# Sliding attention moved ahead of the forget attention in a two-layer hybrid block

## The reference

```
proj = rms_norm(h) @ w_in
fq, fk, fv, ff, cq, ckv, krope, sq, sk, sv, gates = split(proj)
log_decay = cumsum(log_sigmoid(ff + fox_forget_b))
out_a = causal_attention(norm(fq), norm(fk), fv, log_decay)      # forget branch, 8 heads of 64
q, k, v = up-projections of norm(cq), norm(ckv), with rope
out_b = causal_attention(norm(q), norm(k), v)                    # latent branch, 8 heads of 96
out_c = sliding_window(norm(sq), norm(sk), sv, sinks, alibi)     # 8 query heads, 2 shared key heads
y = einsum(branches, w_branch);  merged = sum(sigmoid(gates) * y)
h = h + merged @ w_o
u = rms_norm(h) @ w_up;  h = h + (silu(conv(gate)) * conv(val)) @ w_down
```

## Time and profile before

| | us |
|---|---|
| median of 3 runs | 2052.18 |
| lowest and highest of them | 2051.9 and 2056.09 |
| the profiled execution, its own time | 2050.07 |
| its span in the profile | 2048.3 |
| TensorE busy, share of the span | 1974.3, 96% |
| mean granted TensorE clock | 0.992 |

### The profile page before, as it was taken

One profiled execution on the slowest core, in us unless ns is written; L12 is line 12 of the kernel. 1 busy time (PEld: TensorE's weight loads), 2 busy tenths in 40 slices (PEclk: granted clock), 3 DMA queues, 4 the chain that ended last, 5 costly groups with the idle time before them and its releaser, 6 DMA issues.

```text
span 2048.3 us, 37777 instructions
## 1 busy us (share of the span) xinstructions
PE 1974.3 (96%) x15080; PEld 1876.6 (92%) x15080; DVE 1154.7 (56%) x2137; ACT 766.3 (37%) x1483; POOL 1019.4 (50%) x1306
## 2 busy tenths in 40 slices
PE   7899999999999999999998999999999999999999
PEld 7888898888999999999997888988889999999999
DVE  5665466677455665652256654666774656656411
ACT  5455566555232222220034555665552232222100
POOL 5745544444444444455467555444443445444543
PEclk9999999999999999999999999999999999999999
DMA  4212111111233323323332121111112323232332
GB/s 154 56 50 63 52 44 61 45 50 52 63 105 93 93 83 94 93 83 104 93 115 63 43 63 53 52 52 52 52 42 73 115 83 102 85 100 87 103 94 93
DMA packets 44803, 156.35 MB, mean 76 GB/s; under 512 B 5010, under 2 KB 5266, under 8 KB 44628
## 3 DMA queue, kind: packets, MB, share of 16 engines
q1 hardware_dynamic: 44484, 153.71, 24.8%
q10 hardware_dynamic: 144, 0.22, 0.0%
HBM read 149.58 MB, written 4.26 MB: 75 GB/s over the span
## 4 chain that ended last, share of the span: by engine, by line
PE 80%; DVE 10%; ACT 4%; issue 3%; POOL 2%; DMA 0%; DVEq 0%; ACTq 0%; SPq 0%; POOLq 0%
PE ps L1294 22%; PE ps L1297 21%; PE ps L1299 21%; PE ps L1528 5%; PE ps L1304 3%; DVE osum L1906 2%; PE ps L1435 1%; PE ps L1474 1%; DVE rstd L1619 1%; DVE ps L1876 1%; POOL wl L789 1%; PE ps L1480 1%; PE ps L1500 1%; DVE square L1614 1%; ACT square L987 1%
## 5 line engine op out<-in xcount | busy, mean ns | idle before, releaser
L789 POOL TENSOR_TENSOR wl<-raw,wh 128x256 fp32r<-128x256 f32 x1080 | 797.8, 771 | 723.5 <-DVE wh L1598 714.0
L1294 PE MATMUL ps<-xh,wh 128*128 128x264 f32 (+1 forms) x2880 | 810.6, 303 | 4.9 <-POOL wl L789 2.7
L1297 PE MATMUL ps<-xl,wh 128*128 128x264 f32 (+1 forms) x2880 | 762.9, 285 | 0.0
L1299 PE MATMUL ps<-xh,wl 128*128 128x264 f32 (+1 forms) x2880 | 584.1, 284 | 0.0
L1294 PEld LDWEIGHTS ps<-xh,wh 128*128 128x128 f32 x2880 | 545.5, 189 | 29.0 <-issue 16.0
L1297 PEld LDWEIGHTS ps<-xl,wh 128*128 128x128 f32 x2880 | 545.8, 190 | 15.4 <-issue 6.7
L1299 PEld LDWEIGHTS ps<-xh,wl 128*128 128x128 f32 x2880 | 450.4, 190 | 0.0
L1598 DVE CAST wh<-raw 128x1024 fp32r<-128x1024 f32 x270 | 200.2, 742 | 180.7 <-PE ps L1294 166.2
L1297 PE MATMUL ps<-al,wh 128*128 128x264 f32 (+1 forms) x704 | 184.9, 283 | 0.0
L1294 PE MATMUL ps<-ah,wh 128*128 128x264 f32 (+1 forms) x704 | 183.6, 283 | 0.0
L1898 DVE TENSOR_TENSOR ps<-ps,cst 128x128 f32<-128x128 f32 (+6 forms) x240 | 70.9, 296 | 189.0 <-PE ps L1480 135.8
(11 more groups left out here) (183 smaller groups left out, 3213.3 us busy)
## 6 DMA issues: line engine op xcount, KB each, us to landing
raw<-weights SPq DMA_DIRECT2D x270, 512.0 KB, 3.6
h<-tokens SPq DMA_DIRECT2D x4, 528.0 KB, 6.6
h<-tokens SPq DMA_DIRECT2D x8, 264.0 KB, 5.4
residual<-h SPq DMA_DIRECT2D x8, 264.0 KB, 4.7
h<-residual SPq DMA_DIRECT2D x8, 264.0 KB, 5.9
out<-h SPq DMA_DIRECT2D x8, 256.0 KB, 4.9
cst<-constants SPq DMA_DIRECT2D x1, 1008.0 KB
extra<-positions SPq DMA_DIRECT2D x17, 4.1 KB
```

Of the source, the lines that this page charges most:

```text
L789: ins = nc.gpsimd.tensor_tensor(wl[c % SPLIT][:, part], raw[:, c % RAW, part], wh[c % SPLIT][:, part].bitcast(F32), ALU.subtract)
L1294: a = nc.tensor.matmul(out, a_hi, x_hi[:, sl], start=first, stop=False)
L1297: nc.tensor.matmul(out, a_hi, x_lo[:, sl], start=False, stop=False)
L1299: ins = nc.tensor.matmul(out, a_lo, x_hi[:, sl], start=False, stop=last)
```

## The change

The jobs are reordered: sliding 0 to 3, forget 4 to 7, latent 8 to 11. The first pair of tiles is now `ff` and `sk`, the shared keys of the sliding branch. The gates follow: the sliding branch's gates now lie in `merged`, the forget branch's in the ring `gsb`. `BEGIN`, `ORDER`, the leads and the lags are new numbers. GpSimd fills eight rows of each buffer in place of ten, and buffer 1's fills come 4 blocks after `ff` in place of 24; the rows of ones in `xq` are written by "extras2" for the first two jobs of either branch. The rows of positions for job 0 are loaded at block 3. "kfill" of jobs 0 and 1 waits for the fills of its buffer, and "PVM" of job 0 on ScalarE waits until the decay's rows are made, since both use `osum` and `oraw`.

```diff
--- before.py
+++ after.py
@@ -27,8 +27,8 @@
 BIG = 3.0e38
 PAIRS = HEADS // 2
 FOX, MLA, SWA = range(3)
-JOBS = [(FOX, p) for p in range(PAIRS)] + [(SWA, p) for p in range(PAIRS)] + [(MLA, p) for p in range(PAIRS)]
-FIRST_JOB = {FOX: 0, SWA: PAIRS, MLA: 2 * PAIRS}
+JOBS = [(SWA, p) for p in range(PAIRS)] + [(FOX, p) for p in range(PAIRS)] + [(MLA, p) for p in range(PAIRS)]
+FIRST_JOB = {SWA: 0, FOX: PAIRS, MLA: 2 * PAIRS}
 
 BLK = 8
 CW = BLK * P
@@ -79,14 +79,14 @@
 G_STORED_IN_H = {4: 0, 5: 1, 6: 4, 7: 5}
 Y_LAST = [4, 5, 6, 7, 0, 1, 2, 3]
 STAT_LAG, NORM_LAG = 2, 4
-BEGIN = [65, 94, 122, 156, 192, 221, 250, 280, 319, 354, 391, 436]
-ORDER = ("fk0 fv0 gF0 fq1 fk1 gF1 fk2 fq2 fv1 fk3 fv2 fq3 gF2 sq0 gF3 fv3 sk sv gF4 gF5 sq1 gF6 sq2 gF7 yF0 cq0 cq1 yF1 sq3 yF2 yF3 ckv yF4 mq0 yF5 mv0 yF6 mq1 yF7 gS0 mk0 gS1 mv1 mq2 gS2 gS3 mq3 yS0 mk1 yS1 mq4 gS4 gS5 mq5 yS2 mv2 mk2 gS6 mq6 yS3 gS7 yS4 yS5 mq7 yS6 mk3 gM2 mv3 gM5 gM0 gM4 gM6 yS7 gM1 gM7 gM3")
-M_LEAD, M_STEP, NT_LEAD = 25, 1.8, 4
+BEGIN = [56, 76, 107, 134, 169, 203, 245, 275, 343, 375, 413, 443]
+ORDER = ("sq0 sv sq1 gS0 gS1 sq2 gS2 gS3 sq3 gS4 fk0 gS5 fq0 fv0 gS6 fk1 gS7 fq1 yS0 fv1 yS1 yS2 fk2 yS3 fq2 yS4 yS5 fv2 fk3 yS6 fq3 yS7 fv3 cq0 cq1 ckv gF0 mv0 mq0 gF1 mq1 gF2 mv1 mk0 gF3 yF0 mq2 yF1 gF4 mq3 gF5 mk1 yF2 mq4 gF6 yF3 mq5 gF7 yF4 mv2 yF5 mk2 yF6 mq6 yF7 mq7 gM2 gM1 mk3 gM0 mv3 gM5 gM6 gM4 gM7 gM3")
+M_LEAD, M_STEP, NT_LEAD = 25, 1.9, 3
 ST_HEAD, PV_LAG, ST_END = 7, 2, 13
-ZEROS = 10
-FIRST_LEAD, FIRST_STEP = 18, 1.0
-START = [13, 16, 11, 25, 25, 29, 12]
-LAG = {("dve", "layer stat"): 1, ("dve", "M"): 1, ("dve", "MM"): 1, ("act", "O"): -1, ("pool", "high"): -1, ("act", "head copy"): 1, ("dve", "STM"): -1, ("dve", "decay2"): 2, ("pool", "extras2"): -1, ("dve", "rope"): -1, ("dve", "square low"): 1, ("act", "inverse"): 2}
+ZEROS = 8
+FIRST_LEAD, FIRST_STEP = 18, 0.8
+START = [13, 17, -12, 2, 25, 31, 3]
+LAG = {("dve", "layer stat"): 1, ("dve", "M"): 1, ("dve", "MM"): 1, ("pool", "high"): -1, ("act", "head copy"): 1, ("pool", "extras2"): -1, ("dve", "rope2"): 1, ("act", "kfill"): -1, ("dve", "square low"): -1, ("dve", "decay2"): 1, ("act", "PVM"): -1, ("act", "inverse"): 2, ("dve", "decay"): 1}
 
 
 def constants():
@@ -193,7 +193,7 @@
                 order.append((t, k))
 
     branch = {"F": FOX, "S": SWA, "M": MLA}
-    a, b = tile("ff"), tile("fq", 0)
+    a, b = tile("ff"), tile("sk")
     order.extend((t, k) for k in range(KD) for t in (a, b))
     for name in ORDER.split():
         kind, m = name.rstrip("0123456789"), int("0" + name.lstrip("abcdefghijklmnopqrstuvwxyzFSM"))
...
@@ -241,17 +241,18 @@
                 t.joint = tiles[t.i - 1]
             put(e + STAT_LAG, 3, "stat", t)
             at = e + NORM_LAG
-            job = {"fq": 0, "fk": 0, "sq": PAIRS, "mk": 2 * PAIRS}.get(t.kind)
+            job = {"fq": PAIRS, "fk": PAIRS, "sq": 0, "mk": 2 * PAIRS}.get(t.kind)
             job = t.m + job if job is not None else 2 * PAIRS + t.m // 2 if t.kind == "mq" else None
             if job is not None and job >= 2:
                 at = max(at, BEGIN[job - 2] + ST_END)
             put(at, 6, "newton", t)
             put(at + 1, 6, "norm", t, 0)
+            high_at[job] = at
             if t.kind in ("cq", "mk"):
                 put(at + 2, 6, "norm", t, 1)
             if t.kind == "mq":
                 put(e + 1, 6, "turn", t)
-            put(at + 2 + (START[-1] if t.m == 0 and t.kind == "fq" else 0), 7, "high", t)
+            put(at + 2 + (START[-1] if t.kind == "sk" else 0), 7, "high", t)
             assert next_in_slot[t.i] >= e + STAT_LAG + 1, (t.kind, t.m, next_in_slot[t.i] - e)
         if t.kind in ("fv", "sv", "mv"):
             put(e + 3, 3, *place(("VT", t, 0)))
@@ -266,7 +267,7 @@
                 put(e + at, rank, step, 0)
             for n in range(ZEROS):
                 put(1 + n, 8, "zero", 0, n)
-                put(e + 24 + n, 8, "zero", 1, n)
+                put(e + 4 + n, 8, "zero", 1, n)
             put(4, 9, "zero values")
             put(e + 2, 9, "zero low")
     for i, pairs in ((end_of["g", (FOX, 3)], ((FOX, 0), (FOX, 2))), (end_of["g", (FOX, 7)], ((FOX, 4), (FOX, 6))),
@@ -283,11 +284,12 @@
         elif j > 0:
             put(b - M_LEAD - 9, 4, "extras", j)
             put(b - M_LEAD - 5, 4, "extras2", j)
+        lead, by = (M_LEAD, M_STEP) if j else (FIRST_LEAD, FIRST_STEP)
         if br == SWA:
-            put(b - M_LEAD - 4, 7, "kfill", j, 0)
-            put(b - M_LEAD - 3, 7, "kfill", j, 1)
+            i = min(b - lead - 4, high_at[j])
+            put(i, 7, "kfill", j, 0)
+            put(i, 7, "kfill", j, 1)
         parts = [(e, q) for e in range(2) for q in (("4", "3", "2", "1") if br == SWA else ("4a", "4b", "3", "2", "1"))]
-        lead, by = (M_LEAD, M_STEP) if j else (FIRST_LEAD, FIRST_STEP)
         for n, (e, q) in enumerate(parts):
             put(b - lead + int(n * by), 4, *place(("M", j, e, q)))
         put(b - lead + int(len(parts) * by), 4, *place(("MM", j)))
...
@@ -806,7 +808,7 @@
 
             fills = [(t, lo, HD + lo, lo_e, 0, n, 0) for t, n in ((xq, T), (xk, TK)) for lo, lo_e in ((HD, 0), (0, 1))]
             fills += [(xk, 0, HD, 0, 0, 1, 0), (xk, HD, P, 1, 0, 1, 0), (xk, MQ, MQ + 1, 0, 0, TK, 1),
-                      (xk, 0, 1, 1, 0, TK, 1), (xq, HD, HD + 2, 0, 0, T, 1), (xq, 32, 34, 1, 0, T, 1)]
+                      (xk, 0, 1, 1, 0, TK, 1)]
             assert len(fills) == ZEROS
 
             def zero(i, n):
@@ -882,6 +884,8 @@
                                 nc.gpsimd.tensor_copy(xq[row:row + 2, i, e, :], extra[0:2, 0:T]).then_inc(
                                     pool_step.sem, pool_step.tick((l, "position", j, e)))
                                 began["last"] = (pool_step.sem, pool_step.n)
+                            elif br == FOX and p < 2:
+                                fill(xq, row, row + 2, i, e, 0, T, 1)
                         settled()
                         pool.sem_inc(extras_placed.sem, extras_placed.tick((l, j)))
                     elif s[0] == "ones":
...
@@ -1127,7 +1131,12 @@
                         j, e = s[1], s[2]
                         i, kv = j % 2, JOBS[j][1] // 2
                         src = slice(kv * HD, (kv + 1) * HD)
-                        act.wait_ge(scores_ready.sem, scores_ready.at(l, j - 2, 1, 4))
+                        if j >= 2:
+                            act.wait_ge(scores_ready.sem, scores_ready.at(l, j - 2, 1, 4))
+                        else:
+                            act.wait_ge(zeroed.sem, zeroed.at(l, j))
+                            if l > 0:
+                                act.wait_ge(spilled.sem, spilled.at(l - 1))
                         act.wait_ge(key_low.sem, key_low.at(l, "sk"))
                         own, other = slice(e * HD, (e + 1) * HD), slice((1 - e) * HD, (2 - e) * HD)
                         copy(xk[own, i, e, 1:T + 1], skh[src, :].bitcast(F32))
@@ -1216,6 +1225,8 @@
                     elif s[0] == "PVM":
                         j = s[1]
                         act.wait_ge(meta_done.sem, meta_done.at(l, j))
+                        if j == 0:
+                            act.wait_ge(decay_ready.sem, decay_ready.at(l))
                         if j > 0:
                             act.wait_ge(heads_low.sem, heads_low.at(l, j - 1))
                         bank = banks[s[2]["bank"]]
...
```

28 lines of the change are left out of this document (14 added, 14 removed).

## The result

The changed kernel takes **2109.36 us** (median of 4 runs, 2105.43 to 2112.44), the kernel before 2052.04 in the same comparison. The ratio is 1.0279, with a 95% interval of 1.0257 to 1.03: 57 us slower. The forecast was 2057.3, with a range up to 2067. The side was right, the size was wrong by a factor of ten.

A forecast was written before the change was run, and what follows sets the result against it. TensorE, busy 96% of the span, was taken as the bound. Terms -0.6 - 5.5 + 9.0 + 2.2 = +5.1 on 2050.07 gave 2055.2, raised by the profiled run's 2.1 below median to 2057.3 us; range 2043 to 2067.

The forecast's parts named there:

- The start, layer 0: Blocks up to 56 in layer 0: new waits of 11.2 us, plus 1.7 of low clock.
- the chain to the first scores: Layer 0 start: GpSimd and ScalarE queues delay job 0's first scores to 56.5; TensorE waits 4.7 us.
- the rule on the shared port: Start: two-input VectorE instructions block GpSimd's SBUF reads, so fills stay slow; without it the sum would be -7.6, not -0.6.
- the waits of 3.1 for a maximum behind it and of 2.4 behind rope: Layer 0 start: TensorE waits 3.1 us for maxima behind VectorE's scan, then 2.4 uncovered behind rope and a cast.
- That kind of wait: Start: first scores waiting for GpSimd to place the decay's rows; 7.4 of 7.7 us forecast to go.
- The start, layer 1: Layer 1 start: four copies replace two fills, chain about 1.2 us later, waits 12.4 us, plus 1.7 clock.
- the whole start: Start, both layers: 24.1 us comes and 24.7 goes, net -0.6; bounds -16 to +6.
- rival (a): Start pays, with no decay delaying first scores: -8 to -16 instead of -0.6, total 2042 to 2050; chance 0.26.
- The latent branch's first scores: Latent branch's start: wait for the key's high part goes, with its low clock; -5.5 us, at worst 0.
- The end of attention: Output tiles' fourth block waits 3.5 us per layer for job 11's heads; +9.0 with clock, bounds 6 to 12.
- Crowding: Latent jobs within blocks 343 to 443, and the sliding branch: small waits grow; +2.2 us, bounds -2 to +8.
- rival (d): ScalarE falls behind in sliding jobs, later starts cost wait plus low clock; +10 to +16, 2062 to 2068; chance 0.16.

The follow-up runs named there:

- e1: Changed kernel with VectorE's reciprocals of the four latent pairs cut to 4 of 132 columns; 20.5 us faster than the changed kernel.
- e4: Changed kernel with its last pair four blocks earlier and the last keys' tile two tiles earlier; median 4.6 us slower than the changed kernel, intervals overlapping.
- e11b: Changed kernel with the third latent pair's keys tile 9 blocks earlier, ahead of two forget output tiles; no measurable gain.
- e13: Changed kernel with eight tiles reordered at blocks 378 to 415, two latent gate tiles moved ahead; 8 us faster than the changed kernel.
- e15: Changed kernel with VectorE's reciprocals of the four sliding pairs cut to 4 of 132 columns; 15.9 us faster than the changed kernel.
- e12: Changed kernel with its start mended: decay, scan, rope, second buffer's zeros and first forget values later, shared keys' low half unmoved; 9.7 us faster.
- e8: Old kernel with two of four VectorE reciprocals of each latent pair done three times; 27.6 us slower than the old kernel.
- e18: Changed kernel with VectorE's reciprocals of all twelve pairs cut to 4 columns; 34.0 us faster than the changed kernel.
- e5: Changed kernel with latent tiles from block 305 ordered as in the old kernel and last pairs moved; time not stated, blocks 304 to 490 excess some 124 us.
- e16: Changed kernel with latent tiles earlier and spread, latent pairs at 333, 366, 400, 436, and the start mended; 2126 us.
- e3: Changed kernel with M_STEP and NT_LEAD put back to the old kernel's 1.8 and 4; 2113.81 us.

## Why the prediction was wrong

The terms in the order of the sum, both layers, against the excess of the table above.

- **The start, layer 0: the chain to the first scores right, the terms behind it wrong.** GpSimd's and ScalarE's queues in after:

```profile
34.66 0.88 POOL L879 CAST xk<-extra 2x530 fp32r<-2x530 f32 x1 [0.17 <-DMA extra<-positions]
...
44.39 1.31 POOL L804 CAST xq<-unit 64x528 fp32r<-64x528 f32 x2 [0.17 <-POOL yk L804]
...
47.83 1.74 POOL L924 TENSOR_TENSOR skl<-q,skh 128x528 fp32r<-128x528 f32 x1
```
```profile
49.66 0.65 ACT L974 ACTIVATE xk<-skh 64x528 fp32r<-64x528 f32 x1 [2.77 <-POOL skl L924]
...
53.24 0.73 ACT L1060 ACTIVATE oraw<-osum,prm 8x528 f32<-8x528 f32 x1
...
55.35 1.31 ACT L974 ACTIVATE xq<-q 64x528 fp32r<-64x528 f32 x2
```
```profile
52.47 0.66 PE L1409 MATMUL ps<-cst,vt 128*128 128x128 f32 x4 [2.64 <-DVE vt L1736]
53.70 0.27 PE L1414 MATMUL ps<-cst,vt 128*17 128x128 f32 x1
56.76 0.47 PE L1446 MATMUL ps<-xk,xq 66*128 66x16 f32 x2 [1.33 <-issue]
58.58 0.80 PE L1446 MATMUL ps<-xk,xq 66*128 66x16 f32 x2 [1.35 <-ACT vx L974]
...
76.33 0.47 PE L1446 MATMUL ps<-xk,xq 66*128 66x16 f32 x2 [1.61 <-POOLq L890]
```

The low part was forecast to end at 49.2 (49.57 here), ScalarE's six copies at 53.1 (53.2), the decay at 55.2 (55.3), the first scores at 56.5 (56.76). The four copies took 34.66 to 38.39, 3.7 for 3.9. The five fills were not slow, as I had them (4.2 us) and as I had expected by the rule on the shared port: they took 3.2, and VectorE stood idle beside them for 2.13 of these us:

```profile
46.92 0.71 DVE L1625 TENSOR_TENSOR square<-ssum,square 128x528 f32<-128x528 f32 x1 [2.13 <-ACT square L993]
```

The low part of the key, with VectorE at work beside it, took 1.74 for 1.31, and the queue had begun 0.8 later than I had it; so the close hit on 49.2 is in part luck. The wait of 4.7 us came in two pieces, 2.6 for the values behind the decay on VectorE and 1.3 for the scores, which I had taken for one. Behind it the prediction fails: the scan ended at 61.1, as forecast, but the waits of 3.1 for a maximum behind it and of 2.4 behind rope did not come. In their place stand 1.4 us for ScalarE's copy of the values (58.58) and 1.6 us for the position rows of job 1 on GpSimd (76.33). That kind of wait I had counted as gone (7.4 us). It is back in four pieces of 1.6 to 1.8, 7.1 us in all, for jobs 1 and 3 of each layer. At block 131 comes the wait of 3.6 us for `vt`, which no term of mine holds. Blocks 0 to 304 of layer 0 lose 1.1 us all the same, since blocks 184 to 304 have 9.5 less.
- **The start, layer 1: wrong.** I made it 1.2 us dearer than layer 0. It loses 10.5 us in blocks 0 to 304. The waits there are those of layer 0; the difference is the clock. In the first 184 blocks the granted clock is 0.96 in layer 0 and 0.93 in layer 1, where before has 0.98 and 0.99. Layer 1 in after:

```profile
1066.76:1308.10 241.34, 222.73 (x1528) 202.74 (x1526) 134.00 (x283) 129.15 (x268) 127.95 (x159) 0.93 0.21 62
```

The four other executions with the same first 304 blocks (e1, e4, e11b, e13) have an excess of 77 to 84 us there in layer 0 and 81 to 89 in layer 1, against 80 and 76 in before, so the loss of layer 1 is real and its size moves by some us. e15 takes 10.6 us back in layer 1 and 8.1 in layer 0, e12 9.8 and 3.3. So the whole start is +11.6 and not -0.6, outside both my bounds (-16 to +6) and those of rival (a). It is more than that by what the next term gained, since the latent branch's old wait stood at block 294.
- **The latent branch's first scores: right.** The wait for the keys is gone (timeline of TensorE in after, no bracket), and the clock is 1.00 at 385 us. The size, -5.5, can't be told from the 20.3 us less in blocks 184 to 344, most of which are pairs that stand elsewhere.

```profile
410.29 0.29 PE L1446 MATMUL ps<-xk,xq 96*128 96x264 f32 x1
```

- **The end of attention: right.** Forecast a wait of 3.5 in each layer and +9.0 with the clock. Measured are 3.0 and 3.1 at the fourth block, and +10.0 in blocks 424 to 490:

```profile
607.25 0.39 PE L1305 MATMUL ps<-oth,wh 128*128 128x264 f32 x1 [3.02 <-POOL otl L964]
```

- **Crowding: the step that failed.** I gave it +2.2, with bounds of -2 and +8, "as no single one of them is over 1.5". It is the +37.4 us of blocks 304 to 424, where TensorE's waits went from 10.8 to 35.1 us. The mistake was to bound it by the size of the waits that before has. Small waits in before do not say how far it is from larger ones, and e8 shows that it is not far: 32 us more work, 27.6 us more time. What could have warned me is a comparison that I did not make: VectorE's busy time between blocks against TensorE's undisturbed work (the length of the stretch less the excess). Blocks 344 to 424 of layer 0, before and after (the third number of busy time is VectorE's):

```profile
447.10:543.80 96.70, 93.80 (x672) 85.11 (x672) 65.22 (x137) 45.97 (x95) 42.64 (x49) 1.00 0.20 59
439.76:562.88 123.12, 109.43 (x726) 96.99 (x725) 83.38 (x164) 56.84 (x119) 50.18 (x52) 0.96 0.15 44
```

VectorE has 65.2 us to do beside 80.0 of TensorE's in before, and 83.4 beside 85.4 in after: next to no slack. It is a warning and no price. Before itself carries 77.1 against 81.8 in blocks 304 to 384, at an excess of 20 us where after has 38 in its 80. And e18, with 77.4 against 85.4 in blocks 344 to 424, still has 30. Relieving VectorE gave back 15 of the 37.4 us (e1, e18); so its shortage is shown as a cause of the failed term, and not as the whole of it. I had looked at ScalarE instead, as in rival (d), which had the right sign at a fourth of the size.
- **Rival (d)'s multiplier was right in kind.** "Each later start costs its wait plus a low clock": of the 59.7 us 27.9 are the clock. I had counted 3.4 + 2.0 us for it and 6.4 + 1.7 as gone, so that by my sum the clock would have given 2.7 us back.

How much of the 57 us is settled: 31 to 34 come back when VectorE is relieved behind the pairs (e18). Of the other 24, some 5 are the end. The rest, some 20 in blocks 304 to 424, is not explained: waits for VectorE's queries and maxima and for ScalarE's exponents stay there, and that these are late by where their steps stand, whatever the load (rival P of e1), is not excluded for this part. No run took work from ScalarE, though in e5 and e16 it is the engine whose waits grew, and no layout of mine (e5, e13, e16) lifted the loss without others coming.

## What to carry to other kernels

Where in-order engines feed each other by a table of steps, the mean share of an engine (VectorE 56%) says nothing of what a new order costs: compare, stretch by stretch, each helper's work with that of the engine that must never wait, in the old order and the new, before pricing any single wait. Test how near the edge the kernel stands by adding and removing the same small work in both; if removing brings nothing and adding costs nearly its length, as here, a new order starts without slack. And a wait removed by a table is paid back where the moved steps land, so price the landing too.

## What the runs showed of the hardware

- **In this change a wait cost nearly twice its length.** Right behind the 1.8 and 1.4 us of idle time in the rows at 155 and 510 us TensorE's clock is 0.57, mostly 1.2 GHz. Half of the difference between the two kernels is TensorE working slower, not waiting. The split is not fixed: e3, as slow as after, has a clock of 0.985 in its profile and 112.4 us of waits, so there the clock is 15 us of the loss. In e8 the clock was at 0.990, and of 27.6 us lost it is some 4.
- **VectorE's instructions get longer when GpSimd works beside them.** The same norm of a latent query (L1827 here, L1816 before) takes 0.64 to 0.71 us in all 16 places of before, none of them beside a GpSimd instruction. In after it takes 0.70 or 0.71 in 12 places, 1.11 in the two beside a low part of a chunk and 1.68 in the two beside the low part of the heads (timeline of GpSimd in after):

```profile
527.78 1.57 POOL L964 TENSOR_TENSOR otl<-oraw,oth 128x528 fp32r<-128x528 f32 x1
```

The norm is the row at 528.24 above. The Trainium skill, page "SBUF — State Buffer", section "Who interferes with whom", says that a VectorE instruction with two SBUF inputs and a GpSimd instruction that reads SBUF exclude each other; the trace agrees, here with VectorE as the one that waits. Over the whole run VectorE is busy for 11.5 us longer with the same 2137 instructions. That is no measure of an order, though: in e16, which took 2126 us, it is busy for 1144.4, less than in before.
- **The same work is free or dear by place.** Cutting 25 us of VectorE's reciprocals (20 us of its busy time) in the sliding pairs brought 0.6 us in one order and 15.9 in the other.
